# Around the expert loops of a two-layer trunk: fewer fill products, token sides made earlier, other closing sums

## The chip, the core and the metric

The kernel runs on one core of a Trainium2 chip. The metric is the device time in microseconds (us) of one execution, taken as the median over runs; lower is better.

## What is computed

The reference is a trunk of two layers over 512 tokens of width 1024, all in float32. Cut to what matters here:

```python
def reference(x, ...):
    x = x + sgu_mixer(rmsnorm(x, a_norm), ...)            # layer 0: gated MLP over 128-token blocks
    x = x + hierarchical_moe(rmsnorm(x, m_norm[0]), ...)  # 32 experts, two per token
    k, v, cum = shared_kv(x, kv_norm, kv_w, ...)          # keys, values, forget gates
    x = x + forgetting_attention(rmsnorm(x, b_norm), k, v, cum, ...)   # layer 1
    x = x + hierarchical_moe(rmsnorm(x, m_norm[1]), ...)
    return x

def expert_block(xb, e):                                  # inside hierarchical_moe
    hid = jax.nn.silu(xb @ w1[e]) * (xb @ w3[e])
    return hid @ w2[e]                                    # weighted, added to its tokens' rows
```

Each expert has three matrices of 2 MB (w1, w3, w2), so each layer reads 32 experts of 6 MB.

## The kernel before

`X` (128 partitions x 4 token blocks x 1024) holds the stream. The experts' weights go through three buffers `EB0` to `EB2`; an expert sits in buffer `slot(e)`. The loads of the first three experts are issued before a layer's expert loop. Every later one is issued by SyncE (SP) in `load_later_expert` (L403 to L415): w1 and w3 of expert e once the "up" products of the last item of expert e-3 are done, w2 once its "down" products are. SP waits in program order, and its transfers are served in that order.

An **item** is a slice of up to 32 tokens of one expert; there are 47 in each layer. TensorE runs `expert` (L1472) for each expert, with a loop over its items: up products (L1479), the sums of the item before into its tokens' rows (`move_items`, L1450), the gathering of the next item's tokens (L1468), down products (L1490). ScalarE does the silu (L663) and the weighted output `y_hi` (L666). VectorE multiplies and transposes (L986, L989), adds the moved rows to `X` (L995, `add_items`, which counts `added`), makes the next item's input (L959, L961), the **token sides** (`spread_tokens`, L968 and L971: zeros and ones that say which token rows an item's outputs go to; they are the stationary operand of L1450) and the rest `y_lo` of the weighted output (L1000).

Two places around this loop matter.

*Ahead of the loop* (VectorE, L974 to L983) the sides for token blocks 0 and 1 of the last items, `spread_end`, are made; then a memset counts `added` for the first time, and the loop starts. TensorE's first `move_items` waits for that count.

*After the loop* the outputs of the last two items are still to be added. TensorE's `move(banks, sides)` sums them for two token blocks into four banks (L1450, 32 products), first with `spread_end` for blocks 0 and 1, then with `spread` for blocks 2 and 3, which VectorE makes at L1021 after the last `add_items`. VectorE adds them to `X` (`add_moved`, L1029, counted by `x_moe`). In layer 0 the projection of the keys follows at once: its first weight tile `T_K` comes as one load of 2 MB into `ring[0]`, ScalarE splits it into a rounded part (L622, counted by `w_hi`) and VectorE into the rest (L853, counted by `w_lo`), in quarters; TensorE turns `X` (`turn_stream`, L1352), ScalarE and VectorE split the turned rows (`turned_hi`, L606; `rows_lo`, L843). In layer 1 the rows of blocks 2 and 3 are not added by VectorE: TensorE puts `X` into the banks by products with the identity (`rows_to_bank`, L1530, four column groups), sums on top of them, and ScalarE copies the two blocks out (L825). SP then stores the four blocks of `out` as each is ready (L463 to L466).

`keep_busy(bank, n)` is n products whose result nobody reads (the fill; each shows as two matmuls in the trace). There are 12 between the last-but-one expert and the last (L1526), 8 after the first closing `move` of layer 0 (L1541) and 8 more ahead of the projection of the keys (L1617).

## Time and profile before

| | |
|---|---|
| time, median of 3 runs | 1585.27 us (1583.48 to 1585.3) |
| span of the profiled execution | 1584.0 us |
| TensorE busy | 1476.6 us (93%) |
| VectorE busy | 980.7 us (62%) |
| ScalarE busy | 474.0 us (30%) |
| mean granted TensorE clock | 0.983 of full speed |
| DMA | 461.12 MB, mean 291 GB/s |

The span is the time from the first to the last instruction of one execution; what lies around it is not in it, and the profiled execution has no time of its own beside its span. The median of the timed runs is 1.3 us above that span. A clock of 1.00 in the rows is 2.4 GHz, 0.5 is 1.2 GHz.

### The profile page before, as it was taken

The numbers are of one execution on the slowest core, as the hardware profiler recorded it, in microseconds if no ns is written. First come the engines' busy times: TensorE is split into PE (matmuls) and PEld (weight loads), VectorE is DVE, ScalarE is ACT, GpSimd is POOL, SyncE is SP. The second block draws the span as 40 slices with busy tenths as digits, with TensorE's granted clock in tenths as the row PEclk, the third lists the DMA queues.
The fourth block names the chain that finished last, engine by engine and source line by source line (L and its number), as shares of the span: only waits on it lengthen the run. The fifth ranks groups of instructions, "written<-read, shape, count | busy, mean of one in ns | idle before, by whom it ended". The sixth has DMA issues, their size and how long they took to land.

```text
span 1584.0 us, 45784 instructions
## 1 busy us (share of the span) xinstructions
PE 1476.6 (93%) x18897; PEld 1002.0 (63%) x18898; DVE 980.7 (62%) x2114; ACT 474.0 (30%) x798; POOL 25.8 (2%) x64
## 2 busy tenths in 40 slices
PE   8999999999989989988999999989899897997978
PEld 6788888765555556545778875458655554554545
DVE  5346642377767767765744357852777675675755
ACT  6442221412222222221543355533222221221211
POOL 3000000000000000000000000000000000000000
PEclk9999999999999999998999999999999998999989
DMA  6331332989999999999431322125899999999996
GB/s 220 119 106 54 107 106 69 389 331 429 429 428 427 430 428 427 429 430 428 179 106 55 121 80 81 40 74 245 357 389 427 429 429 429 427 429 429 428 428 277
DMA packets 55482, 461.12 MB, mean 291 GB/s; under 512 B 4496, under 2 KB 4640, under 8 KB 30848
## 3 DMA queue, kind: packets, MB, share of 16 engines
q1 hardware_dynamic: 51728, 453.00, 69.0%
q10 hardware_dynamic: 2192, 4.23, 0.8%
q0 software_dynamic: 1504, 3.07, 0.7%
q8 instruction: 42, 0.69, 0.2%
q14 instruction: 16, 0.13, 0.0%
HBM read 458.15 MB, written 2.13 MB: 291 GB/s over the span
## 4 chain that ended last, share of the span: by engine, by line
PE 72%; DMA 22%; DVE 4%; issue 2%; SPq 0%; ACT 0%; DVEq 0%; ACTq 0%
DMA EB<-in_m_w 22%; PE ps L1479 15%; PE ps L1317 10%; PE ps L1319 10%; PE ps L1318 10%; PE ps L1468 7%; PE ps L1490 6%; PE ps L1450 4%; PE ps L1705 2%; PE ps L1740 1%; PE ps L1759 1%; PE ps L1774 1%; PE ps L1592 1%; PE ps L1313 1%; PE ps L1379 1%
## 5 line engine op out<-in xcount | busy, mean ns | idle before, releaser
L1479 PE MATMUL ps<-EB,SCR 128*32 128x256 f32 x6016 | 364.4, 397 | 72.5 <-DMA EB<-in_m_w 59.7
L1479 PEld LDWEIGHTS ps<-EB,SCR 128*32 128x32 f32 x6016 | 195.7, 114 | 233.4 <-issue 105.1
L995 DVE TENSOR_TENSOR X<-X,ps 128x1024 f32 x188 | 221.1, 1218 | 28.9 <-PE ps L1450 28.9
L1319 PE MATMUL ps<-EB_r 128*128 128x512 f32 x512 | 200.2, 391 | 0.0
L1468 PE MATMUL ps<-H,SCR 128*32 128x256 f32 x3072 | 185.6, 382 | 0.0
L1490 PE MATMUL ps<-EB,SCR 128*32 128x256 f32 x3008 | 179.5, 379 | 0.0
L666 ACT ACTIVATE SCR_r<-ps,SCR 128x256 f32 x94 | 44.5, 474 | 443.4 <-PE ps L1490 443.4
L986 DVE TENSOR_TENSOR SCR<-SCR,ps 128x128 f32<-128x128 f32 x94 | 37.0, 393 | 211.6 <-ACT SCR L663 211.6
L1490 PEld LDWEIGHTS ps<-EB,SCR 128*32 128x32 f32 x3008 | 97.7, 110 | 64.5 <-DVE SCR L989 0.4
L1318 PE MATMUL ps<-EB_r 128*128 128x512 f32 x352 | 137.5, 391 | 0.0
L1468 PEld LDWEIGHTS ps<-H,SCR 128*32 128x32 f32 x3072 | 90.4, 110 | 62.1
L1317 PE MATMUL ps<-EB_r,H_r 128*128 128x512 f32 x320 | 126.8, 396 | 1.4 <-DVE EB L1084 1.0
L1450 PEld LDWEIGHTS ps<-SCR_r 32*128 32x128 f32 x3136 | 99.8, 184 | 44.6 <-issue 44.6
L1318 PE MATMUL ps<-EB_r,H_r 128*128 128x512 f32 x320 | 124.7, 390 | 0.0
L1450 PE MATMUL ps<-SCR_r 32*128 32x256 f32 x3136 | 119.6, 290 | 3.7 <-DVE col L983 2.1
L663 ACT ACT_TABLE_LOAD x94 | 120.6, 1283 | 2.0 <-ACT SCR L659 0.3
L1319 PEld LDWEIGHTS ps<-EB_r 128*128 128x128 f32 x512 | 96.3, 188 | 20.5
L663 ACT ACTIVATE SCR<-ps 128x128 f32<-128x128 f32 x94 | 26.1, 278 | 245.3 <-PE ps L1479 245.3
L971 DVE SCALAR_TENSOR_TENSOR SCR_r<-SCR,item_slot,SCR_r 128x256 fp32r<-128x256 f32 x192 | 84.6, 482 | 14.8 <-DVE SCR_r L968 14.7
L857 DVE TENSOR_TENSOR EB_r<-EB,EB_r 128x1024 fp32r<-128x1024 f32 x56 | 65.1, 1220 | 38.2 <-ACT EB_r L625 38.2
L1317 PE MATMUL ps<-EB_r 128*128 128x512 f32 x192 | 77.4, 403 | 3.6 <-DVE EB_r L1288 3.5
L1318 PEld LDWEIGHTS ps<-EB_r 128*128 128x128 f32 x352 | 66.5, 189 | 12.6
(280 smaller groups left out, 1667.0 us busy)
## 6 DMA issues: line engine op xcount, KB each, us to landing
EB<-in_m_w SPq DMA_DIRECT2D x192, 2048.0 KB, 26.9
EB<-in_a_w_in SPq DMA_DIRECT2D x7, 2048.0 KB, 8.2
EB<-in_a_w_out SPq DMA_DIRECT2D x4, 2048.0 KB, 7.9
EB<-in_kv_w SPq DMA_DIRECT2D x4, 2048.0 KB, 12.6
EB<-in_b_w_qg SPq DMA_DIRECT2D x4, 2048.0 KB, 7.9
EB<-in_b_w_out SPq DMA_DIRECT2D x2, 2048.0 KB, 9.4
X<-in_x SPq DMA_DIRECT2D x4, 512.0 KB, 6.9
EB<-in_a_w_in SPq DMA_DIRECT2D x4, 512.0 KB, 9.7
```

The lines of the kernel that those rows point to most:

```text
L663: a.activation(silu, ps[0][:, 0:P], ACT.Silu).then_inc(m["silu"], 1)
L666: a.activation(y_parts[:, bass.ds(n & 1, 1), 0, :], ps[2][:, CW:2 * CW].unsqueeze(1), ACT.Copy, scale=slot_w[:, bass.ds(n, 1)]).then_inc(m ...
L857: v.tensor_tensor(ring_lo[j][:, 2 * q:2 * q + 2, :], ring[j][:, 2 * q:2 * q + 2, :], ring_hi[j][:, 2 * q:2 * q + 2, :].bitcast(F32), ALU.s ...
L971: v.scalar_tensor_tensor(dst[:, i, :], toks[1], item_slot[:, bass.ds(items[i] + 2, 1)], dst[:, i, :].bitcast(F32), ALU.is_equal, ALU.add). ...
L995: add = v.tensor_tensor(X_t, X_t, moved[1][:, :, t, :], ALU.add)
L1317: mm(o, left[0], right[0], start=start, stop=False)
L1318: mm(o, left[0], right[1], start=False, stop=False)
L1319: return mm(o, left[1], right[0], start=False, stop=stop)
L1450: last = mm(moved[banks][:, g, t, :], sides[rows, i, t * P:(t + 1) * P], y_parts[rows, i, k, :], start=first and i == 0 and k == 0, stop=( ...
L1468: last = mm(ps[1][g * CAP:(g + 1) * CAP, 0:CW], S[:, c, :], H[:, c * D + g * CW:c * D + (g + 1) * CW], start=c == 0, stop=c == NT - 1)
L1479: last = mm(ps[0][g * CAP:(g + 1) * CAP, 0:2 * P].rearrange("p (w n) -> p w n", w=2), xT[:, k, :], w13_sb[s][:, :, k, g * P:(g + 1) * P], ...
L1490: last = mm(ps[2][g * CAP:(g + 1) * CAP, CW:2 * CW], hidT[:, c, :], w2_sb[s][:, c, g * CW:(g + 1) * CW], start=c == 0, stop=c == KE - 1)
```

## The change

Six edits go together. (1) The fill ahead of the last expert has 2 products where it had 12, and the fill after layer 0's first closing `move` 6 where it had 8. (2) The sides for blocks 2 and 3 are made ahead of the loop, behind `spread_end`, into a place of their own (`spread_late`, in the buffer `gain`). (3) In layer 0 VectorE adds block 0 only after the first quarter of `T_K`'s rest, and block 1 only after the rest of block 0's turned rows. (4) `T_K` comes in four loads of 512 KB, each with its own semaphore. (5) In layer 1 the first closing `move` goes to the other four banks and no longer waits for `added`; only two column groups of blocks 2 and 3 are put into banks by identity products, and the other two are added by VectorE while ScalarE copies the first out. (6) Blocks 2 and 3 are stored by column halves.

```diff
+        spread_late = gain_r[:, 0:2 * CW].rearrange("p (i n) -> p i n", i=2)
...
-            for i in range(T_K, T_K + 2):
-                sp.dma_start(ring[i % 2], tiles[i]).then_inc(tile_loaded[i % 2], 16)
+            for q in range(4):
+                sp.dma_start(ring[0][:, 2 * q:2 * q + 2, :], tiles[T_K][:, 2 * q:2 * q + 2, :])\
+                    .then_inc(first_loaded[q], 16)
+            sp.dma_start(ring[1], tiles[T_K + 1]).then_inc(tile_loaded[1], 16)
...
-            for t in range(NT):
-                sp.wait_ge(*((x_moe, NT + t + 1) if t < 2 else (x_copied, t - 1)))
+            for t in range(2):
+                sp.wait_ge(x_moe, NT + t + 1)
                 sp.dma_start(out[0, t * P:(t + 1) * P, :], X[:, t, :]).then_inc(stored, 16)
+            for h, ready in ((1, (x_copied, 1)), (0, (x_moe, NT + 3))):
+                sp.wait_ge(*ready)
+                sp.dma_start(out[0, 2 * P:T, h * COL:(h + 1) * COL].rearrange("(t p) n -> p t n", p=P),
+                             X[:, 2:4, h * COL:(h + 1) * COL]).then_inc(stored, 16)
...
             act.wait_ge(end_moved, 4)
-            for t in range(2):
-                a.activation(X[:, 2 + t, :].rearrange("p (g n) -> p g n", g=CG), moved[0][:, :, t, :], ACT.Copy)\
-                    .then_inc(x_copied, 1)
+            a.activation(X[:, 2:4, COL:D].rearrange("p t (g n) -> p g t n", g=2), moved[1][:, 2:4], ACT.Copy)\
+                .then_inc(x_copied, 1)
...
                 spread_tokens(spread_end, 0, (total - 2 + (total & 1), total - 1 + (total & 1)), lambda ins, i: then(ins),
                               end_spread)
+                spread_tokens(spread_late, 1, (total - (total & 1), total - 2 + ((total + 1) & 1)),
+                              lambda ins, i: then(ins), end_spread)
                 dve.wait_ge(slot_w_done, 2 * l + 2)
                 v.memset(cn[:, 0:1], 0.0).then_inc(m["added"], 1)
...
                 add_items(total - 1)
-                spread_tokens(spread, 1, (total - (total & 1), total - 2 + ((total + 1) & 1)), lambda ins, i: then(ins),
-                              end_spread)
                 rest_of_rows(total - 1)
...
                 dve.wait_ge(end_moved, 2 * l + t // 2 + 1)
+                if l == 1 and t == 2:
+                    X_g = X[:, 2:4, 0:COL].rearrange("p t (g n) -> p g t n", g=2)
+                    v.tensor_tensor(X_g, X_g, moved[1][:, 0:2], ALU.add).then_inc(x_moe, 1)
+                    return
...
-            for t in range(2):
-                add_moved(0, t)
             split_tile(T_K, 0, 1)
+            add_moved(0, 0)
             rows_lo("kv", 0)
+            add_moved(0, 1)
             split_tile(T_K, 1, 4)
...
-                keep_busy(0, 12, CW)
+                keep_busy(0, 2, CW)
                 expert(slot(NE - 1), (NE - 1) // NBUF + 1, start_of(NE - 1), total, True)
...
-                pe.wait_ge(m["added"], total + 1)
-                if l == 1:
-                    for g in (0, 1, 3):
-                        rows_to_bank(g)
+                if l == 0:
+                    pe.wait_ge(m["added"], total + 1)
+                pe.wait_ge(end_spread, 4 * l + 4)
                 pe.wait_ge(m["y_hi"], total + 1)
                 pe.wait_ge(m["y_lo"], total + 1)
-                pe.wait_ge(end_spread, 4 * l + 2)
-                move(1, spread_end).then_inc(end_moved, 1)
+                move(1 - l, spread_end).then_inc(end_moved, 1)
                 if l == 0:
-                    keep_busy(0, 8)
+                    keep_busy(0, 6)
                     turn_stream(0)
                     pe.wait_ge(x_moe, 2)
-                if l == 1:
-                    rows_to_bank(2)
-                pe.wait_ge(end_spread, 4 * l + 4)
-                move(1 - l, spread, first=l == 0).then_inc(end_moved, 1)
+                    move(1, spread_late).then_inc(end_moved, 1)
+                    return
+                pe.wait_ge(m["added"], total + 1)
+                for g in range(2, CG):
+                    mm(moved[1][:, g, :, :], ident[:, :], X[:, 2:4, g * CW:(g + 1) * CW], start=True, stop=False)
+                move(1, spread_late, 2).then_inc(end_moved, 1)
```

Three places in the order of instructions show what moves (after the change line numbers are 14 to 18 higher). VectorE ahead of layer 0's loop, before the change:

```order
L968 TENSOR_SCALAR SCR_r<-SCR,item_slot 128x256
L968 ISA [waits dve_step]
L968 TENSOR_SCALAR SCR_r<-SCR,item_slot 128x256
L971 SCALAR_TENSOR_TENSOR SCR_r<-SCR,item_slot,SCR_r 128x256 [waits dve_step]
L971 SCALAR_TENSOR_TENSOR SCR_r<-SCR,item_slot,SCR_r 128x256
L983 MEMSET col 128x1 [waits slot_w_done]
```

The same place after the change:

```order
L985 SCALAR_TENSOR_TENSOR SCR_r<-SCR,item_slot,SCR_r 128x256
L982 ISA
L982 TENSOR_SCALAR gain_r<-SCR,item_slot 128x256
L982 REGISTER_ALU [waits dve_step]
L982 REGISTER_ALU
L982 ISA
L982 TENSOR_SCALAR gain_r<-SCR,item_slot 128x256
L985 SCALAR_TENSOR_TENSOR gain_r<-SCR,item_slot,gain_r 128x256 [waits dve_step]
L985 SCALAR_TENSOR_TENSOR gain_r<-SCR,item_slot,gain_r 128x256
L999 MEMSET col 128x1 [waits slot_w_done]
```

Four more instructions, with two waits of VectorE on itself, stand between `spread_end` and the memset that TensorE waits for. VectorE behind layer 0's loop, before (from the sides after the last `add_items` on; L853 is the weight tile's rest, L843 the turned rows'):

```order
L968 TENSOR_SCALAR SCR_r<-SCR,item_slot 128x256
L971 SCALAR_TENSOR_TENSOR SCR_r<-SCR,item_slot,SCR_r 128x256 [waits dve_step]
L971 SCALAR_TENSOR_TENSOR SCR_r<-SCR,item_slot,SCR_r 128x256
L1000 ISA [waits moe0_y_hi]
L1000 ISA
L1000 SCALAR_TENSOR_TENSOR SCR_r<-ps,SCR,SCR_r 128x256
L1029 TENSOR_TENSOR X<-X,ps 128x1024 [waits end_moved] x2
L853 SCALAR_TENSOR_TENSOR EB_r<-EB,cols,EB_r 128x512 [waits w_hi]
L853 SCALAR_TENSOR_TENSOR EB_r<-EB,cols,EB_r 128x512
L843 TENSOR_TENSOR EB_r<-ps,H_r 128x4x128 [waits kv_ht] x2
```

And after:

```order
L1016 SCALAR_TENSOR_TENSOR SCR_r<-ps,SCR,SCR_r 128x256
L867 SCALAR_TENSOR_TENSOR EB_r<-EB,cols,EB_r 128x512 [waits w_hi]
L867 SCALAR_TENSOR_TENSOR EB_r<-EB,cols,EB_r 128x512
L1047 TENSOR_TENSOR X<-X,ps 128x1024 [waits end_moved]
L857 TENSOR_TENSOR EB_r<-ps,H_r 128x4x128 [waits kv_ht] x2
L1047 TENSOR_TENSOR X<-X,ps 128x1024 [waits end_moved]
```

The sides are gone; the add of block 1 now stands behind the rest of block 0's turned rows. TensorE at the end of layer 1, before:

```order
L1530 MATMUL ps<-X,ident 128x512 [waits moe1_added]
L1530 MATMUL ps<-X,ident 128x512 x2
L1450 MATMUL ps<-SCR_r 128x256 [waits end_spread,moe1_y_lo,moe1_y_hi]
L1450 MATMUL ps<-SCR_r 128x256 x31
L1530 MATMUL ps<-X,ident 128x512
L1450 MATMUL ps<-SCR_r 128x256 [waits end_spread]
L1450 MATMUL ps<-SCR_r 128x256 x31
```

And after:

```order
L1550 REGISTER_ALU [waits end_spread]
L1468 MATMUL ps<-SCR_r 128x256 [waits moe1_y_lo,moe1_y_hi]
L1468 MATMUL ps<-SCR_r 128x256 x31
L1561 MATMUL ps<-X,ident 128x512 [waits moe1_added]
L1561 MATMUL ps<-X,ident 128x512
L1468 MATMUL ps<-SCR_r,gain_r 128x256 x32
```

Two of four identity products are gone, and the first closing sums stand ahead of them.

## Rows read from the trace of the kernel before

**Rows 1.** Page, chain of work that ended last: shares of the span by engine

```profile
PE 72%; DMA 22%; DVE 4%; issue 2%; SPq 0%; ACT 0%; DVEq 0%; ACTq 0%
```

**Rows 2.** Timeline, layer 0's loop opening: start, us, engine, line, operands, count [idle before]

```profile
325.92 0.35 DVE L968 TENSOR_SCALAR SCR_r<-SCR,item_slot 128x256 fp32r<-128x256 f32 x1 [0.34 <-DVE SCR L979]
...
326.94 0.88 DVE L971 SCALAR_TENSOR_TENSOR SCR_r<-SCR,item_slot,SCR_r 128x256 fp32r<-128x256 f32 x2
...
327.99 1.22 PE L1450 MATMUL ps<-SCR_r 32*128 32x256 f32 x32 [1.07 <-DVE col L983]
```

**Rows 3.** Stretches: us, busy PE PEld DVE ACT POOL, PEclk, DMA share, GB/s

```profile
344.00:346.00 2.00, 2.00 (x48) 1.18 (x40) 0.77 (x3) 0.37 (x2) 0.00 (x0) 1.00 0.04 16
```

**Rows 4.** DMA issues at 345.75, 717.84, 721.99, 749.71, 1529.67: KB, us to landing

```profile
EB<-in_m_w SPq DMA_DIRECT2D x1, 2048.0 KB, 7.4
...
EB<-in_m_w SPq DMA_DIRECT2D x1, 2048.0 KB, 38.2
...
EB<-in_m_w SPq DMA_DIRECT2D x1, 2048.0 KB, 39.0
...
EB<-in_kv_w SPq DMA_DIRECT2D x1, 2048.0 KB, 16.8
...
EB<-in_m_w SPq DMA_DIRECT2D x1, 2048.0 KB, 37.7
```

**Rows 5.** Timeline, layer 0's last expert and the handover to the keys

```profile
754.32 2.94 PE L1313 MATMUL ps<-tri_in,tri 128*128 128x128 f32 x24
...
762.03 1.93 PE L1490 MATMUL ps<-EB,SCR 128*32 128x256 f32 x32
...
764.29 0.47 ACT L666 ACTIVATE SCR_r<-ps,SCR 128x256 f32 x1 [3.09 <-PE ps L1490]
...
766.39 0.48 DVE L1000 SCALAR_TENSOR_TENSOR SCR_r<-ps,SCR,SCR_r 128x256 f32 x1
766.51 2.56 ACT L622 ACTIVATE EB_r<-EB,cols 128x512 fp32r<-128x512 f32 x4 [1.75 <-DMA EB<-in_kv_w]
...
767.28 1.22 PE L1450 MATMUL ps<-SCR_r 32*128 32x256 f32 x32 [1.59 <-DVE SCR_r L1000]
...
768.55 2.35 DVE L1029 TENSOR_TENSOR X<-X,ps 128x1024 f32<-128x1024 f32 x2 [1.69 <-PE ps L1450]
...
770.32 1.04 PE L1352 MATMUL ps<-ident,X 128*128 128x128 f32 x8
...
770.82 1.41 DVE L853 SCALAR_TENSOR_TENSOR EB_r<-EB,cols,EB_r 128x512 fp32r<-128x512 f32 x2
...
771.29 1.22 PE L1450 MATMUL ps<-SCR_r 32*128 32x256 f32 x32
```

**Rows 6.** Timeline, a later block turned on TensorE and its rest on VectorE

```profile
782.73 1.04 PE L1352 MATMUL ps<-ident,X 128*128 128x128 f32 x8
...
783.99 1.29 DVE L843 TENSOR_TENSOR EB_r<-ps,H_r 128x512 fp32r<-128x512 f32 x2 [0.43 <-ACT H_r L606]
```

**Rows 7.** Timeline, end of layer 1

```profile
1567.57 1.94 PE L1490 MATMUL ps<-EB,SCR 128*32 128x256 f32 x32
...
1571.16 2.84 PE L1530 MATMUL ps<-X,ident 128*128 128x512 f32 x6
...
1575.08 1.13 PE L1530 MATMUL ps<-X,ident 128*128 128x512 f32 x2
...
1576.45 3.25 SPq L465 DMA_DIRECT2D out_x<-X  x4
...
1577.41 1.94 ACT L825 ACTIVATE X<-ps 128x1024 f32<-128x1024 f32 x2 [7.11 <-PE ps L1450]
```

**Rows 8.** Timeline of TensorE, up products after three waits for weights

```profile
682.78 3.66 PE L1479 MATMUL ps<-EB,SCR 128*32 128x256 f32 x64 [3.31 <-DMA EB<-in_m_w]
...
726.82 6.23 PE L1479 MATMUL ps<-EB,SCR 128*32 128x256 f32 x64 [4.89 <-DMA EB<-in_m_w]
...
1445.13 5.35 PE L1479 MATMUL ps<-EB,SCR 128*32 128x256 f32 x64 [3.32 <-DMA EB<-in_m_w]
```

**Rows 9.** Stretch behind the wait that ends at 726.82, columns as in rows 3

```profile
725.00:730.00 5.00, 3.18 (x32) 1.62 (x36) 0.00 (x0) 0.00 (x0) 0.00 (x0) 0.53 1.01 429
```

More of the change, by code:

```diff
@@ L84, in trunk @@
         SCR, SCR_r = sb_split("SCR", [P, 5 * D])
-        gain = sb("gain", [P, D])
+        gain, gain_r = sb_split("gain", [P, D])
         h_tok = H[:, :].rearrange("p (t g k r) -> p t g k r", t=NT, g=CG, k=KD)
@@ L348, in split_no, with tile_loads @@
             return i if i <= T_G else i - (T_WO - T_G - 1)
+        def tile_loads(i):
+            if i == T_K:
+                return None
+            return i // 2 + i % 2 - (i % 2 == 0 and i > T_K)
         H_LO = {"a": 0, "kv": 2 * NT}
@@ L616, in split_hi @@
             def split_hi(j, loads, q0=0, q1=4, scale=None):
-                act.wait_ge(tile_loaded[j], 16 * loads)
+                if loads is not None:
+                    act.wait_ge(tile_loaded[j], 16 * loads)
                 for q in range(q0, q1):
+                    if loads is None:
+                        act.wait_ge(first_loaded[q], 32)
                     if scale is not None:
@@ L628, in split_tile @@
             def split_tile(i, q0=0, q1=4):
-                split_hi(i % 2, i // 2 + i % 2, q0, q1, weight_gain(i))
+                split_hi(i % 2, tile_loads(i), q0, q1, weight_gain(i))
             def moe_act(l, ready):
@@ L750, in scale_gate @@
             def scale_gate(i, k):
-                act.wait_ge(tile_loaded[i % 2], 16 * (i // 2 + i % 2))
+                act.wait_ge(tile_loaded[i % 2], 16 * tile_loads(i))
                 a.activation(ring[i % 2][:, k, :], ring[i % 2][:, k, :], ACT.Copy, scale=b_gain[:, k:k + 1])\
@@ L1027, in add_moved @@
                 dve.wait_ge(end_moved, 2 * l + t // 2 + 1)
+                if l == 1 and t == 2:
+                    X_g = X[:, 2:4, 0:COL].rearrange("p t (g n) -> p g t n", g=2)
+                    v.tensor_tensor(X_g, X_g, moved[1][:, 0:2], ALU.add).then_inc(x_moe, 1)
+                    return
                 X_t = X[:, t, :].rearrange("p (g n) -> p g n", g=CG)
-                v.tensor_tensor(X_t, X_t, moved[1 - l * (t // 2)][:, :, t % 2, :], ALU.add).then_inc(x_moe, 1)
+                v.tensor_tensor(X_t, X_t, moved[1 - l][:, :, t % 2, :], ALU.add).then_inc(x_moe, 1)
             def router_blocks(l, add):
@@ L1302, in _ @@
             moe_dve(1)
-            for t in range(2):
+            for t in range(3):
                 add_moved(1, t)
@@ L1441, in moe_pe, with move @@
                    start=False, stop=True).then_inc(lists_out, 1)
-                def move(banks, sides, first=True):
+                def move(banks, sides, opened=CG):
                     for t in range(2):
@@ L1450, in move @@
                                     last = mm(moved[banks][:, g, t, :], sides[rows, i, t * P:(t + 1) * P],
-                                              y_parts[rows, i, k, :], start=first and i == 0 and k == 0,
-                                              stop=(first or t == 1) and i == 1 and k == 1)
+                                              y_parts[rows, i, k, :], start=g < opened and i == 0 and k == 0,
+                                              stop=(g < opened or t == 1) and i == 1 and k == 1)
                     return last
@@ L1525, in moe_pe @@
                 total = pe.value_load(n0_i[0:1, NE:NE + 1], min_val=NE, max_val=MAX_ITEMS)
-                keep_busy(0, 12, CW)
+                keep_busy(0, 2, CW)
                 expert(slot(NE - 1), (NE - 1) // NBUF + 1, start_of(NE - 1), total, True)
-                def rows_to_bank(g):
-                    mm(moved[0][:, g, :, :], ident[:, :], X[:, 2:4, g * CW:(g + 1) * CW], start=True, stop=False)
-                pe.wait_ge(m["added"], total + 1)
-                if l == 1:
-                    for g in (0, 1, 3):
-                        rows_to_bank(g)
+                if l == 0:
+                    pe.wait_ge(m["added"], total + 1)
+                pe.wait_ge(end_spread, 4 * l + 4)
                 pe.wait_ge(m["y_hi"], total + 1)
                 pe.wait_ge(m["y_lo"], total + 1)
-                pe.wait_ge(end_spread, 4 * l + 2)
-                move(1, spread_end).then_inc(end_moved, 1)
+                move(1 - l, spread_end).then_inc(end_moved, 1)
                 if l == 0:
-                    keep_busy(0, 8)
+                    keep_busy(0, 6)
                     turn_stream(0)
                     pe.wait_ge(x_moe, 2)
-                if l == 1:
-                    rows_to_bank(2)
-                pe.wait_ge(end_spread, 4 * l + 4)
-                move(1 - l, spread, first=l == 0).then_inc(end_moved, 1)
+                    move(1, spread_late).then_inc(end_moved, 1)
[4 more added lines that the diff above has]
+                move(1, spread_late, 2).then_inc(end_moved, 1)
             pe.wait_ge(const_ready, 5)
```

## The prediction

> **What bounds the kernel now.** I read the chain of waits first, and in it the share of each engine: 72% TensorE and 22% DMA [rows 1]. That mixes two regimes, so I went to the expert loops and listed every weight load with its issue and landing. The reader is to see three things there. First, the loads run dry once, near the start: in 344 to 346 us the DMA engines are 4% busy [rows 3], because the load of the fifth expert's w1 is issued only at 345.75, when TensorE has freed its buffer, and lands at 353.1. Second, from there on they never run dry: 28 experts follow with three loads each, and the last, w2, is issued at 721.99 and lands 39.0 later, at 761.0 [rows 4]. That is 83 steps in 407.9 us, 4.9 us for each 2 MB, without a hole. Third, TensorE is a little faster than that and waits again and again for weights (waits of 3.3 to 4.9 us in [rows 8]). So between 345.75 and the last expert the loop is bound by the stream of loads. What delays 345.75 delays the end of the layer by as much, and work saved on TensorE inside buys nothing. Layer 1 has the same pattern: its last w2 lands at 1529.67 + 37.7 = 1567.4 and the last down products start at 1567.57 [rows 4, 7]. Between the loops, and ahead of 345.75, TensorE is the bound.
>
> **The change part by part**, in the times of the profiled execution.
>
> *Sides made ahead of the loop.* `spread_end` takes VectorE from 325.92 to 327.82, 1.9 us for four instructions, and TensorE's first `move_items` starts at 327.99, held by the memset behind them [rows 2]. The new four have the same shapes and the same waits on themselves, so 1.9 us more stand ahead of that memset. Behind it on VectorE wait the first item's hidden products (L986) and so the down products too; nothing in this stretch hides them, since TensorE already waited 1.07 us there. TensorE is 1.9 us late at 345.75, and the stream of loads, dry at that moment, starts 1.9 us late. Cost +1.9 in each layer. Bounds: 0 if something ahead of 345.75 took it up, 2.3 if the registers for the items' numbers add to it.
>
> *Fill ahead of the last expert, layer 0.* 24 matmuls take 2.94 us from 754.32 on [rows 5]; 20 of them go, 2.45 us. But w3 of this expert, issued at 717.84, lands at 756.0, and w2 at 761.0 [rows 4]; both are now 1.9 later. The fill would end at 754.3 + 1.9 + 0.5 = 756.7, the up products wait for w3 until 758.0 (they began at 757.2), and the down products for w2 until 763.0, where they began at 762.03 [rows 5]. Net +0.95: of the 2.45 us saved 0.95 arrive.
>
> *Sides gone behind the loop.* y_hi ends at 764.76 + 0.95 = 765.7, and the rest L1000 follows it at once, at 765.75 where it stood at 766.39 behind the sides. The first closing move starts 0.65 earlier, at 766.65 [rows 5].
>
> *Handover to the keys.* The first quarter of `T_K` must be split before VectorE adds block 0. The whole tile lands 16.8 after 749.71, at 766.5, 5.5 behind w2 [rows 4]; a quarter takes 1.4, so the first is there at 761.0 + 1.4 + 1.9 = 764.3 and does not hold ScalarE, which is busy until 765.7. ScalarE's two pieces take half of 2.56, to 767.1; VectorE's two 1.41, to 768.5; the add of block 0 half of 2.35, to 769.7 [rows 5], the very time of before. TensorE turns block 0 at 769.8 to 770.1, before at 770.32 because of the fill. From the start of such turning to the end of VectorE's rest of the turned rows it takes 782.73 to 785.28, 2.55 us [rows 6]: 772.3 to 772.6. Only now comes the add of block 1, 1.2 more, and 0.4 behind it the second closing move (before: add ended 770.90, move 771.29 [rows 5]): 773.9 to 774.2. The eight fill products and the keys follow as before. So the keys start 2.6 to 2.9 us late, I take +2.7; this is the sum of layer 0 with its opening in it. The two fill products taken out are worth nothing: TensorE waits for the add instead. The later quarters, blocks and loads keep their cover, the keys' products, which start late themselves; of five SP issues in place of two none is waited for.
>
> *Last expert of layer 1.* Its down products start 0.17 after w2 lands: the fill was worth nothing there, 0 to -0.1.
>
> *End of layer 1.* Four identity products (eight matmuls) take 2.84 + 1.13 = 3.97 [rows 7]; two go: TensorE ends 1.95 earlier, near 1575.4. ScalarE copies once where it copied twice, 1.94 in all, so its half is out near 1576.4. VectorE adds blocks 0 and 1 from 1572.5 to 1574.8 and its half of the others from 1575.4 to 1576.6. The last store was issued at about 1576.45 + 3.25 - 0.35 = 1579.35; now near 1577.0. Gain 2.3; bounds 1.9 (TensorE's part alone) and 2.9 (with all of one copy). Rows of 2 KB where they were 4 KB are inside these bounds: `T_K` comes in rows of 2 KB at 5.5 us for 2 MB against 4.9, 0.15 for a store of 512 KB.
>
> *The clock.* In the handover TensorE now stands idle from about 769.3 to 769.9 and from 770.9 to 774.0, 3.6 us in 4.7, with eight short products between. After a wait of 3.31 us the up products took 3.66 us, after one of 3.32 they took 5.35, and after one of 4.89 they took 6.23 [rows 8]; behind that last one the granted clock is 0.53 over 5 us, so nearly all of it at 1.2 GHz [rows 9]. A fall costs 1.7 to 2.6 us where TensorE is the bound. I take one fall, in the handover, at the smaller price, 1.7, because the products behind this gap are long and dense. At each loop opening the wait grows from 1.07 to 3.0 us, shorter than both the 3.31 that kept the clock and the 3.32 that lost it; I leave the clock up there. Ahead of layer 1's last expert the 2.45 us of fill turn into idle time, shorter still.
>
> The rows put the fall here by the length of the gap alone. The Trainium skill ("TensorE: Matmul & The Clock Gate", section "Why this matters for your kernels") asks that idle gaps between bursts of products be kept short, since otherwise the half clock comes back; it speaks against taking fill away at all. By it the handover and perhaps both openings fall: +2.3 + 3 x 1.7 = +7.4. By the row that kept the clock none falls: +2.3. The trace shows both sides of it, one wait of 3.31 kept and one of 3.32 lost.
>
> **Sum.** +2.7 (layer 0) + 1.9 (opening of layer 1) + 0 (last expert) - 2.3 (end) = +2.3; with the fall +4.0. Against the span of 1584.0 that is 1588.0; the median of the runs shown stands 1.3 above the span, so 1589.3.
>
> **The rivals.**
> *More falls of the clock* (0.22): an opening falls too. For it: 3.0 us of idle is near 3.3. Against it: both examples are longer. With one more +5.7, 1591.0; with two +7.4, 1592.7.
> *No fall* (0.16): for it the wait of 3.31. +2.3, 1587.6.
> *The openings are hidden* (0.10; the other side). If the 1.9 us do not reach the issue at 345.75, the last w2 lands at 761.0 as before, the down products start 0.9 earlier instead of later, and the keys start at +0.8; then +0.8 + 0 - 2.3 = -1.5, with a fall +0.2: 1583.8 to 1585.5. It decides from where less than about half of the 1.9 arrives at 345.75. Against it: TensorE has no idle time to give between 329 and 345 but the wait for VectorE.
> *The handover costs nothing and the openings little* (0.09): VectorE's new order overlaps better than the rows say; down to -4, 1581.3.
> *As forecast* (0.40): 1588.0 to 1590.5. About 0.03 is left for none of these.
>
> **How the numbers follow.** What a measurement of this kernel can tell from no change is about 0.2%, 3.2 us. Slower by more: most of the forecast (0.33), more falls (0.22), a little of no fall (0.03) and of the rest (0.02): 0.60. Within: the remainder of the forecast (0.07), of no fall (0.13), the hidden openings and the rest (0.11): 0.31. Faster: 0.09. The range 1585.3 to 1592.2 leaves out the faster cases and the case of three falls; the likeliest case's own range is 1588.0 to 1590.5.
>
> **What would show it.** Right: VectorE's first loop memset about 1.9 us later after `spread_end`, the load that ended the dry stretch 1.9 us later against the loop's start, landings 4.9 us apart up to the end; TensorE waiting for a DMA ahead of both last experts; an idle stretch of about 3 us between the turning of block 0 and the second closing move in layer 0, and half clock behind it; four identity matmuls less and the last store about 2.3 us earlier against layer 1's last down products. Wrong: the issue near 345.75 at its old distance from the loop's start, a second closing move in layer 0 not later than before, or a gain at the end under 1.9 or over 2.9.

## The result, and the profile after

The changed kernel takes 1595.09 us (median of 4 runs, 1589.9 to 1598.76), the kernel before beside it 1584.65 (1583.48 to 1585.3): ratio 1.0064, 95% interval 1.0052 to 1.0076. In the first group of experiments it was 1593.65 against 1584.65, ratio 1.0055 (1.0042 to 1.0069). It is slower by 10.4 us here and by 9.0 there, where the prediction said 4 and ended its range at 1592.2. The profiled execution took 1589.9 us, with a span of 1588.1; it is the fastest of the four, which matters below.

The end of the page's chain of waits, shares by engine (before: [rows 1]), shows more time behind transfers and less behind TensorE:

```profile
PE 68%; DMA 25%; DVE 4%; issue 2%; ACT 0%; SPq 0%; DVEq 0%; ACTq 0%
```

Timeline of the changed kernel at the opening of layer 0's loop (start, us, engine, line, operands, count, idle before), first VectorE, then TensorE:

```profile
327.02 0.88 DVE L985 SCALAR_TENSOR_TENSOR SCR_r<-SCR,item_slot,SCR_r 128x256 fp32r<-128x256 f32 x2
327.82 0.34 DVE L982 TENSOR_SCALAR gain_r<-SCR,item_slot 128x256 fp32r<-128x256 f32 x1
...
328.88 0.88 DVE L985 SCALAR_TENSOR_TENSOR gain_r<-SCR,item_slot,gain_r 128x256 fp32r<-128x256 f32 x2
...
329.71 0.06 DVE L999 MEMSET col<- 128x1 f32 x1
```

```profile
323.34 3.66 PE L1497 MATMUL ps<-EB,SCR 128*32 128x256 f32 x64
329.93 2.08 PE L1468 MATMUL ps<-SCR_r 32*128 32x256 f32 x32 [2.93 <-DVE col L999]
331.94 2.42 PE L1486 MATMUL ps<-H,SCR 128*32 128x256 f32 x32
...
336.88 3.66 PE L1497 MATMUL ps<-EB,SCR 128*32 128x256 f32 x64 [0.79 <-issue]
```

The second set of sides (`gain_r`) lies between 327.82 and 329.76, and the memset behind it (L999) ends at 329.77, where it ended at 327.83 before: 1.9 us, as predicted. TensorE's first `move_items` starts at 329.93 after 2.93 us of idle time ([rows 2]: 1.07). It takes 2.08 us and the gather behind it 2.42, where 1.22 and 1.93 are usual: the clock fell. The stretch 329 to 334 shows it (granted clock 0.66), and the DMA share of 346 to 349 (0.00) shows the dry loads, which restart at 349.04 instead of 345.75 (columns as in [rows 3]; the DMA share and GB/s come last):

```profile
346.00:349.00 3.00, 3.00 (x64) 1.67 (x54) 1.95 (x6) 1.47 (x3) 0.00 (x0) 1.00 0.00 0
329.00:334.00 5.00, 4.07 (x64) 2.92 (x68) 3.10 (x7) 0.00 (x0) 0.00 (x0) 0.66 0.92 393
```

The opening of layer 1, with nearly the same idle time (2.92 us), kept the clock. The last row is the last expert of layer 1, whose up products waited 2.39 us for w3 behind the two fill products and took 5.35 us, partly at half clock, instead of 3.66; before, they stood behind the fill without such a wait:

```profile
1139.85 1.22 PE L1468 MATMUL ps<-SCR_r 32*128 32x256 f32 x32 [2.92 <-DVE col L999]
...
1567.87 5.35 PE L1497 MATMUL ps<-EB,SCR 128*32 128x256 f32 x64 [2.39 <-DMA EB<-in_m_w]
```

Handover of layer 0, TensorE and VectorE (before: [rows 5]):

```profile
764.48 1.93 PE L1508 MATMUL ps<-EB,SCR 128*32 128x256 f32 x32
...
769.79 1.21 DVE L1047 TENSOR_TENSOR X<-X,ps 128x1024 f32<-128x1024 f32 x1
...
771.06 1.09 PE L1370 MATMUL ps<-ident,X 128*128 128x128 f32 x8 [0.18 <-DVE X L1047]
...
772.45 1.29 DVE L857 TENSOR_TENSOR EB_r<-ps,H_r 128x512 fp32r<-128x512 f32 x2 [1.44 <-ACT H_r L618]
...
773.65 1.21 DVE L1047 TENSOR_TENSOR X<-X,ps 128x1024 f32<-128x1024 f32 x1
...
774.92 1.22 PE L1468 MATMUL ps<-SCR_r,gain_r 32*128 32x256 f32 x32 [2.77 <-DVE X L1047]
```

Block 0 is added in 769.79 to 771.00, turned, its rest made to 773.74, and only then is block 1 added (to 774.86). The second closing move (L1468 at 774.92) waited 2.77 us for it, and the keys start at 777.88, 13.40 behind the down products (before 12.21). The end of layer 1, whose down products start at 1574.38 (before: [rows 7]):

```profile
1579.19 1.98 PE L1561 MATMUL ps<-X,ident 128*128 128x512 f32 x4
...
1581.10 1.22 PE L1468 MATMUL ps<-SCR_r,gain_r 32*128 32x256 f32 x32
1582.38 1.02 ACT L839 ACTIVATE X<-ps 128x1024 f32<-128x1024 f32 x1 [5.25 <-PE ps L1468]
1582.38 1.22 DVE L1044 TENSOR_TENSOR X<-X,ps 128x1024 f32<-128x1024 f32 x1 [0.72 <-PE ps L1468]
```

One group of identity products of 1.98 us stands where 3.97 stood, one copy (L839) where two stood. From the down products to the end of the span it is 13.67 us, before 16.48.

### The profile page after: what moved, and what is told of

Same layout as the page of the kernel before. It is cut to its first block, busy times and chain, and to the rows that moved or that the text cites. A ratio compares the mean times of both kernels' runs of the same rounds, so it can differ in the third digit from the quotient of the medians.

```text
span 1588.1 us, 45690 instructions
## 1 busy us (share of the span) xinstructions
PE 1474.6 (93%) x18849; PEld 998.2 (63%) x18850; DVE 982.2 (62%) x2115; ACT 473.1 (30%) x797; POOL 25.9 (2%) x64
## 4 chain that ended last, share of the span: by engine, by line
PE 68%; DMA 25%; DVE 4%; issue 2%; ACT 0%; SPq 0%; DVEq 0%; ACTq 0%
DMA EB<-in_m_w 25%; PE ps L1497 14%; PE ps L1335 10%; PE ps L1337 10%; PE ps L1336 10%; PE ps L1486 6%; PE ps L1508 5%; PE ps L1468 4%; PE ps L1720 2%; PE ps L1755 1%; PE ps L1774 1%; PE ps L1789 1%; PE ps L1607 1%; PE ps L1397 1%; PE ps L1383 0%
## 5 line engine op out<-in xcount | busy, mean ns | idle before, releaser
L1468 PEld LDWEIGHTS ps<-SCR_r 32*128 32x128 f32 x3072 | 98.7, 185 | 46.6 <-issue 46.6
L1468 PE MATMUL ps<-SCR_r 32*128 32x256 f32 x3072 | 118.4, 291 | 6.7 <-DVE col L999 5.8
```

The costliest lines, as they stand in the source:

```text
L1468: last = mm(moved[banks][:, g, t, :], sides[rows, i, t * P:(t + 1) * P], y_parts[rows, i, k, :], start=g < opened and i == 0 and k == 0, s ...
```

## Where the time is, stretch by stretch

All traces were cut at the same points of the timeline: "start" is layer 0's first up products; "opening" from there to the second item's; "last" from the landing of the last w2 to the last down products; "handover" from these to the first keys product; "keys" from there to layer 1's first up products; "end" from layer 1's last down products to the end of the span. The first row is the kernel before in us, the others the difference to it. Not shown is the loop from the second item to the last landing: 427.05 to 427.51 us in all 20 traces and both layers. So the loop took the same time whatever stood around it, and never carried a difference.

| trace | start | opening 0 | last 0 | handover | keys | opening 1 | last 1 | end | span |
|---|---|---|---|---|---|---|---|---|---|
| before | 323.26 | 10.33 | 1.04 | 12.21 | 355.42 | 10.28 | 0.20 | 16.48 | 1584.0 |
| after, profiled | +0.1 | +3.2* | -1.0 | +1.2 | 0 | +1.8 | +1.6* | -2.8 | +4.0 |
| r1_after | +0.2 | +3.3* | +0.6* | +2.8* | +1.0 | +1.8 | +1.6* | -2.8 | +7.9 |
| r2_after | +1.1 | +3.5* | +0.7* | +2.8* | +1.1 | +1.8 | 0 | -2.8 | +7.9 |
| r3_after | +1.0 | +3.5* | +0.7* | +2.8* | +1.2 | +1.9 | +1.6* | -2.8 | +9.4 |
| r4_after | +0.8 | +3.4* | +0.7* | +2.8* | +1.0 | +1.8 | 0 | -2.8 | +7.6 |
| e1_sides | +1.0 | +3.4* | -0.9 | -0.9 | +0.1 | +3.6* | 0 | 0 | +6.1 |
| e2_fills | +0.7 | 0 | +0.7* | -0.5 | +1.1 | 0 | -0.1 | 0 | +1.5 |
| e3_end | -0.4 | 0 | 0 | -0.2 | -1.6 | 0 | 0 | -1.3 | -3.9 |
| e4_order | +1.1 | 0 | -0.9 | +5.4* | -1.6 | 0 | 0 | 0 | +3.6 |
| e5_back_sides | +1.3 | -0.1 | -0.9 | +2.1 | -1.7 | 0 | +1.5* | -1.5 | +0.5 |
| e6_back_order | +0.6 | +3.4* | +0.7* | -1.9 | 0 | +3.4* | +1.6* | -2.8 | +4.7 |
| e7_back_fill | +1.0 | +3.5* | -0.9 | +3.7* | +0.2 | +3.4* | 0 | -2.8 | +7.7 |
| e8_mem | +1.0 | -0.1 | +0.7* | +2.6* | 0 | -0.1 | +1.6* | -2.8 | +2.3 |
| e11_open_fill | +1.5 | +1.8 | -0.9 | +2.7* | +1.3 | +1.9 | +1.5* | -2.8 | +6.8 |
| e13_fill_and_order | +0.4 | +3.3* | -0.9 | -1.9 | -1.7 | +3.5* | 0 | -2.8 | -0.7 |
| e10_best | +0.4 | -0.1 | -0.9 | -1.9 | -1.6 | -0.1 | 0 | -2.8 | -7.6 |
| e12_best_sides_back | +1.4 | -1.2 | -0.9 | -0.6 | +1.1 | -1.2 | +1.0 | -1.5 | -2.1 |
| e14_sides_in_gap | +0.8 | -1.1 | -0.9 | -1.9 | +1.2 | -1.2 | +1.0 | -2.8 | -4.8 |
| e15_sides_in_gap_8 | +0.4 | -1.2 | -0.9 | -1.9 | +1.2 | -1.2 | +0.8 | -2.8 | -5.9 |

A star: the clock fell in that stretch (in "end", where it falls in every trace once TensorE is done, none is set). "Start" and "keys" lie outside the change and move by up to 1.5 and 1.7 us in kernels of every kind; what moves "keys" is a fall near 1056 us that is absent (353.8 us), short (355.4) or twice as long (356.5). So the parts are read in the other columns, with the medians as a check on them. Each row is one execution. In "last 0" the -0.9 needs no edit: e4 has it too, whose code is that of the kernel before up to there, and so have e1, e7, e10 and e13 with all 12 fill products. The traces of before and e3 are the ones in which TensorE came 1.0 us late for the last w2.

## The experiments

Theory A: the mechanism of the prediction holds, and the clock falls at more places than one. Its rival in the first group, B: the stream of loads itself runs slower than before. Later rivals stand with their runs. "Before" stands at 1584.6 to 1585.0 us in every group of runs.

**The whole change and its parts, each alone on the kernel before.**

> The changed kernel again, to see how wide its own times are and where a slower execution loses. Theory A (late loop openings, late handover): the profiled spans scatter with the number of falls of the TensorE clock, 1.2 to 1.7 us each, at five places (both openings, both last experts, the handover): 1588 to 1594 us of device time. Theory B (something outside the changed places is slower, such as the rate of the loads): the last weight load of a layer lands more than 408 us after the first one behind the dry stretch, and times reach 1599.

> The kernel before with the sides of blocks 2 and 3 made ahead of the loop, nothing else. Theory A: the loads restart 1.9 us later in each layer, layer 0 gives 1.6 back behind its loop, layer 1 nothing: +2.2 us with the clock up, up to +6 with a fall at each opening. Rival (the openings are hidden): 0 to -1.6 us. Theory B': the fills alone make the loss: this one is within 1 us of before.

> The kernel before with the shorter fills alone (12 to 2, 8 to 6). Theory A: layer 0 gains 0.9 to 1.2 us (the rest of the removed 2.45 us is a wait for weights), layer 1 nothing: -1.2 to -0.9 us with the clock up. Theory B' (the fills held the clock up): +1 to +5 us, the spread of times wider than before, low clock over the last expert's products.

> The kernel before with layer 1's closing sums, copies and stores of the change alone. Theory A: -2.3 us (bounds -1.9 and -2.9). Rival: the four stores bunch and the last lands no earlier: 0 to -1.

e1 adds the two parts of the diff on `spread_late`, e2 is `keep_busy(0, 2, CW)` and `keep_busy(0, 6)`, e3 edits (5) and (6). Measured: r1 1593.65; e1 1591.12, ratio 1.0036 (1.0023 to 1.005); e2 1586.86, 1.001 (1.0001 to 1.0019); e3 1582.71, 0.9988 (0.9979 to 0.9997). The sides alone bring +6.5 us, the fills +2.2, the end -1.9. B falls: the loop between the second item and the last landing takes the same in all. e1 came out half a us above A's range, with a fall at each opening. e2 contradicts A (-1.2 to -0.9) and fits its rival, that the fills held the clock: its trace has one fall at the touched places, in layer 0's last expert, after a wait of 2.17 us. The touched stretches of that trace sum to only +0.1, though; the rest of its +1.5 lies mostly in "start" and "keys", so e2 does not show how much of the +2.2 the fill makes. e3 is at the edge of A's bounds by its time (-1.9), but in its trace the end gains only 1.3. In the changed kernel it gains 2.8, because the sides no longer stand in its way: in e3 the first closing sum, which now goes ahead of the identity products, stands idle for 1.24 us and starts (1569.91) once VectorE has made `y_lo` (1569.81) behind the sides; before, the identity products covered that. So the sides ahead are worth 1.5 at the end once the closing sums are the new ones, and cost 7 at the openings (e1; 5.2 on average in the changed kernel).

The order of VectorE alone is the fourth part:

```diff
-            for t in range(2):
-                add_moved(0, t)
             split_tile(T_K, 0, 1)
+            add_moved(0, 0)
             rows_lo("kv", 0)
+            add_moved(0, 1)
```

> The kernel before with one part only, VectorE's order at the handover (the first key quarter's low part, the add of block 0, the turned rows, the add of block 1). Theory A: the second closing sum starts 2.6 to 3.2 us later behind the first's, down products to the first keys product 14.3 to 15.3 us where they took 12.21, more by 1.5 with a fall of the clock: 1587 to 1589 us. Rival (the keys' start moves, but the later key tiles are reached by their loads at the same time, so that it is given back): the keys start later and layer 1's loop starts as before, 1585.0 us.

1589.6 us, ratio 1.0031 (1.0019 to 1.0043), a little above A. Handover 17.58 us, 5.4 more than before, with a fall in it. Layer 1's first up products start 3.9 us later than before, so it is not given back. The handover is also longer than A's 15.3 plus 1.5: in this trace ScalarE waits 2.53 us for `T_K`, which still comes as one load here, and the add of block 0 stands behind its first quarter. In the changed kernel, where `T_K` comes in four loads, ScalarE does not wait there. No run tests edit (4), the four loads, by itself. Timeline of e4_order, TensorE:

```profile
767.17 1.22 PE L1450 MATMUL ps<-SCR_r 32*128 32x256 f32 x32 [1.33 <-DVE SCR_r L1000]
...
771.41 1.09 PE L1352 MATMUL ps<-ident,X 128*128 128x128 f32 x8 [1.04 <-DVE X L1029]
775.27 2.03 PE L1450 MATMUL ps<-SCR_r 32*128 32x256 f32 x32 [2.77 <-DVE X L1029]
777.23 2.77 PE L1313 MATMUL ps<-tri_in,tri 128*128 128x128 f32 x16
```

**Each part undone in the changed kernel.** e5 makes the late sides behind `add_items(total - 1)` again, e6 restores the old order above, e7 is

```diff
-                keep_busy(0, 2, CW)
+                keep_busy(0, 12, CW)
```

and e8 leaves all work in place but lets TensorE go first:

```diff
+                dve.wait_ge(slot_w_done, 2 * l + 2)
+                v.memset(cn[:, 0:1], 0.0).then_inc(m["added"], 1)
                 spread_tokens(spread_end, 0, (total - 2 + (total & 1), total - 1 + (total & 1)), lambda ins, i: then(ins),
                               end_spread)
                 spread_tokens(spread_late, 1, (total - (total & 1), total - 2 + ((total + 1) & 1)),
                               lambda ins, i: then(ins), end_spread)
-                dve.wait_ge(slot_w_done, 2 * l + 2)
-                v.memset(cn[:, 0:1], 0.0).then_inc(m["added"], 1)
```

> The changed kernel, but the sides of blocks 2 and 3 (kept in the gain's tile) are made behind the last item's adds again, as before. Theory A (the sides ahead of the loop make a wait of about 2.9 us in each opening, which costs 1.8 us and in most executions 1.5 us more for the lost clock): both openings come back to 10.3 us from first to second up products, that is 3.3 to 6.9 us less; the last second sides then stand ahead of the closing sums again, 0.7 us at the handover and up to 1.5 us at the end; in all 1587 to 1590 us. Rival B (fewer fill products and the new order of VectorE carry the loss): 1591 to 1594 us.

> The changed kernel, with VectorE's order at the handover as before (two closing adds, then the first key quarter's low part and the rows). Down products of the last expert to the first keys product took 14.98 and 13.40 us with the new order and 6 fill products, 11.36 us with the old order, 8 fill products and sides ahead. If the order causes it: 11.4 to 12.0 us there and 1590.5 to 1592 us in all. If the two fill products less cause it: it stays at 13.4 to 15.0 and the time stays within 0.5 us of the changed kernel's 1593.65.

> The changed kernel with 12 fill products ahead of the last expert instead of 2. Theory A: the wait of 2.4 us for the last first half loses the clock in the last expert of either layer in most executions (up products 5.35 us instead of 3.7), with the fills back the down products start 0.2 us after the last load in layer 1 and at most 1.0 in layer 0: 0.7 to 2.5 us less, 1591.2 to 1593 us. Rival: those products are hidden behind the load either way, no change from 1593.65.

> The changed kernel, but VectorE's memset, which releases the first item's moved rows on TensorE, stands ahead of both makings of sides instead of behind them. Theory A (what costs in the opening is TensorE's wait for that release): TensorE goes from the up products to the move and the next gather without a gap, no fall of the clock there, openings at 10.3 to 12.1 us and the whole at 1587 to 1590.5 us. Rival (VectorE's own 1.9 us delays the first item's hidden rows): openings stay at 12.1 us and only the clock's part comes back, 1590 to 1592.5.

The differences here are to r1's 1593.65, which was measured in another group. e5 1587.62 (ratio 1.002, 1.0009 to 1.0031): openings back, -6.0 us. e6 1589.38 (1.0022, 1.0013 to 1.0032): -4.3, below the 1590.5 to 1592 expected; the handover takes 10.28, so the order costs 3.1 us there without a fall (13.40) and 4.7 with one (14.98), and the two fill products less are no part of it. Timeline of e6_back_order, TensorE: the second move follows the turning without a wait.

```profile
770.11 1.22 PE L1468 MATMUL ps<-SCR_r 32*128 32x256 f32 x32
771.26 1.60 PE L1331 MATMUL ps<-tri_in,tri 128*128 128x128 f32 x12
772.70 1.05 PE L1370 MATMUL ps<-ident,X 128*128 128x128 f32 x8
773.79 1.22 PE L1468 MATMUL ps<-SCR_r,gain_r 32*128 32x256 f32 x32
```

e8 1588.1 (1.0012, 1.0003 to 1.0021): -5.6 us. Both openings are at 10.2 with VectorE's eight instructions still there. Timeline of e8_mem, TensorE, layer 0:

```profile
324.21 3.66 PE L1497 MATMUL ps<-EB,SCR 128*32 128x256 f32 x64
327.80 1.22 PE L1468 MATMUL ps<-SCR_r 32*128 32x256 f32 x32
328.95 1.93 PE L1486 MATMUL ps<-H,SCR 128*32 128x256 f32 x32
331.32 1.93 PE L1508 MATMUL ps<-EB,SCR 128*32 128x256 f32 x32 [0.43 <-DVE SCR L1005]
334.40 3.66 PE L1497 MATMUL ps<-EB,SCR 128*32 128x256 f32 x64 [1.15 <-DVE SCR L975]
```

The rival, that VectorE's own 1.9 us delay the hidden rows, falls as it stood: what costs the 1.8 us and the fall is TensorE's wait for the memset. Once TensorE may go ahead, the move and the gather (3.1 us) cover most of VectorE's work. What is left are TensorE's waits for VectorE in these rows (0.43 and 1.15 us); where the second sides are not ahead of the loop and the memset stands first (e12), the opening takes 9.1, so they still cost 1.1 there.

e7 missed: 1593.4 (1.0054, 1.0039 to 1.0068), where 1591.2 to 1593 was expected. The last experts did come back (-0.9 and 0), but the clock now fell in layer 1's opening and for longer in the handover. A rival remained, that these products are worth nothing; e13 restores order and fill together, so that nothing falls behind them. Beside it stand three more traces of the changed kernel.

> The changed kernel with VectorE's old order at the handover and 12 fill products ahead of the last expert; against the run with the old order alone (1589.38 us) it tells what the 10 products are worth where nothing falls behind them. Theory A: their removal costs 0.7 us in layer 0 and 1.6 in layer 1 through the clock, so 1587.0 us (1586.3 to 1588). Rival (with them put back, the changed kernel came to 1593.4 and not to 1591.4, so they are worth nothing): 1589.4 us.

> The changed kernel again, one trace more. In two traces of it the clock fell in two openings of four, in the handover once of two, and in the last expert three times of four. If falls are what stands between the profiled 1589.9 and the median of 1593.65: about 3 to 4 falls at these five places, 1592 to 1596 us, each fall dearer by 1.2 to 1.8 us than the same stretch without one.

> The changed kernel, a fourth trace: 3 to 4 falls of the clock at the five places (two openings, two last experts, the handover), 1592 to 1596 us; with fewer falls it should be nearer 1590.

> The changed kernel, a fifth trace: 3 to 4 falls of the clock at the five places (two openings, two last experts, the handover), 1592 to 1596 us; with fewer falls it should be nearer 1590.

e13 1587.86 (1.002, 1.0011 to 1.0029), 1.5 below e6: inside A's range, though smaller than its 2.4. The intervals of the two overlap, so the times alone do not decide against the rival; the traces do, since the up products of both last experts take 5.35 us in e6 and 3.66 in e13. In all 20 traces the clock never fell in a last expert behind 8 or 12 fill products (20 cases), and it fell in 14 of 20 cases behind 2. The three further traces came to 1593.73, 1595.24 and 1593.48 with 3, 4 and 3 falls at the five places, against 2 in the profiled 1589.9. Stretches of r3_after behind three of its falls (opening, last expert, handover):

```profile
331.00:336.00 5.00, 5.00 (x76) 3.01 (x80) 3.04 (x5) 0.00 (x0) 0.00 (x0) 0.66 1.00 423
761.00:766.00 5.00, 5.00 (x64) 2.69 (x60) 0.00 (x0) 0.09 (x1) 0.00 (x0) 0.66 0.98 390
778.00:783.00 5.00, 5.00 (x44) 4.74 (x38) 3.39 (x6) 1.11 (x2) 0.00 (x0) 0.66 0.00 0
```

**Is it the idle time or the moment?** e11 lays fill into the openings' wait (`fill` is 10 for the first expert, 0 for the others), with everything else as it is:

```diff
                         last.then_inc(m["up"], 1)
+                        if fill:
+                            pe.wait_ge(m["y_hi"], n + 1)
+                            pe.wait_ge(m["y_lo"], n + 1)
+                            keep_busy(2, fill, CW)
                         move_items(n)
```

> The changed kernel with 10 fill products (2.45 us) laid into the wait that the second sides made in each opening, in a bank that nobody reads there, behind the first expert's up products. VectorE's work and the wait's end stay as they are. Theory A (the opening costs 1.8 us for VectorE's four instructions and 1.5 us more because TensorE's idle time of 2.9 us loses the clock): both openings take 12.1 us from first to second up products with no fall of the clock, where they took 13.5 to 13.9 in most traces; 1590.3 to 1592.3 us. Rival (the clock falls there whether TensorE is idle or not): openings stay at 13.5 us, no change from 1593.65.

1592.03 (1.004, 1.0027 to 1.0054), 1.6 under r1 but with overlapping intervals; the trace is clearer, though it is one. Both openings take 12.15 and keep the clock, where layer 0's lost it in all nine traces that have the bare wait of 2.9 us; the wait for the memset (+1.8) stays. Timeline of e11_open_fill, TensorE, layer 0:

```profile
324.73 3.66 PE L1497 MATMUL ps<-EB,SCR 128*32 128x256 f32 x64
328.32 2.50 PE L1331 MATMUL ps<-tri_in,tri 128*128 128x128 f32 x20
331.32 1.22 PE L1468 MATMUL ps<-SCR_r 32*128 32x256 f32 x32 [0.50 <-DVE col L999]
332.47 1.93 PE L1486 MATMUL ps<-H,SCR 128*32 128x256 f32 x32
```

**A version that keeps what was good.** e10 is the changed kernel with the edits of e6, e7 and e8 together; e12 is e10 with e5's. e14 is e10 with both sets of sides moved from ahead of the loop to

```diff
                     select(n + 2, m, 0, lambda ins, k: link(ins, k + 2))
+                spread_tokens(spread_end, 0, (total - 2 + (total & 1), total - 1 + (total & 1)), lambda ins, i: then(ins),
+                              end_spread)
+                spread_tokens(spread_late, 1, (total - (total & 1), total - 2 + ((total + 1) & 1)),
+                              lambda ins, i: then(ins), end_spread)
                 gate_item(total - 1)
```

and e15 has `keep_busy(0, 8, CW)` there besides.

> The changed kernel with the three losses taken out: the memset ahead of both sides, 12 fill products ahead of the last expert again, and VectorE's old order at the handover; the sides ahead of the loop, 6 fill products at the handover and the new end of layer 1 stay. Theory A, by the stretches measured so far: openings 10.2 us (as before), last experts as before, down products to keys 10.3 us (1.9 less), end 13.7 us (2.8 less): 4.7 us under the kernel before, 1580.3 us, between 1579.5 and 1581.5. Rival (the parts hide one another's cost, and the gain at the handover comes back as a wait for the key tiles): 1582.2 us, the end's gain alone.

> The kernel of the run before this one (label e10_best), but with the sides of blocks 2 and 3 made behind the last adds again. If those sides ahead of the loop are worth something once the opening doesn't wait for them: handover 0.7 us longer and end 1.5 us longer than there, 1582.0 to 1583.0 us. Rival: within 0.5 us of it.

> The kernel of label e10_best, but all eight instructions that make the four sides stand behind the expert loop on VectorE, ahead of the last item's hidden rows, where VectorE waits 4.1 to 4.4 us for ScalarE (from 755.9 to 760.3 in e10_best's trace; eight instructions take 3.8). Theory A (the sides cost only where somebody waits): openings 9.1 us as with one set behind (1.1 less than in e10_best), handover and end as in e10_best; in layer 1 about 1.0 of it is given back at the last expert, where TensorE with its 12 fill products is itself late for the load; 1578.0 to 1579.8 us. Rival: the hidden rows of the last expert come late behind them, 1580.5 or more.

> As label e14_sides_in_gap, with 8 fill products ahead of the last expert instead of 12. Theory A: the four products less (0.98 us) end the fill about when the last first half has landed in layer 1, so 0.5 to 1.0 us less than e14_sides_in_gap, 1577.3 to 1579 us, with the clock up because the idle time there stays under 1.5 us. Rival: the shorter fill loses the clock in the last expert as 2 products do, 0.7 to 1.6 us more.

e10 1580.54 (0.9972, 0.9962 to 0.9983), as A summed it. e12 1581.75 (0.9981, 0.9972 to 0.999): between the two; by the traces the sides ahead win 1.3 us at handover and end each and lose 1.1 at each opening, but in layer 1 that loss costs next to nothing, since in e12 its last expert stands 1.0 longer behind the load. The intervals of e10 and e12 overlap.

e14 1580.97 (0.9975, 0.9964 to 0.9986) missed its range by 1.2. The openings gained 1.1 each and layer 1's last expert gave 1.0 back, with TensorE late for its own loads, both as expected; against e10's trace the touched stretches sum to -1.0. But its median is 0.4 above e10's, and no run shows why: what is longer in its trace are "start" (0.4), the two loops (0.5) and "keys" (2.9), none of which the edit touches. e15 1578.82 (0.996, 0.9946 to 0.9973) has the lowest median, 5.9 us under before, with an interval that overlaps those of e10 and e14. Its trace has no fall in an opening, a last expert or the handover. Of the 1.0 in layer 1's last expert only 0.2 came back: TensorE is no longer late there, but its down products wait 0.61 us for VectorE's hidden rows, which stand behind the sides. So the rival of e14 is partly true here, and the four products less explain little of the 2.1 us between the two medians.

Timeline of e14_sides_in_gap, VectorE, where it waited 4.36 us in e10's trace:

```profile
756.13 0.35 DVE L982 TENSOR_SCALAR SCR_r<-SCR,item_slot 128x256 fp32r<-128x256 f32 x1 [0.18 <-issue]
...
760.05 0.40 DVE L998 TENSOR_TENSOR SCR<-SCR,ps 128x128 f32<-128x128 f32 x1 [0.17 <-ACT SCR L678]
```

## Why the prediction was wrong

*The bound, right.* From the second item to the last landing it took 427 us in every trace, so what delays the loads' restart delays the layer.

*Openings, half right.* +1.9 for VectorE's four instructions: measured +1.8 where the clock stayed (layer 1, five of five traces). e8 shows this to be TensorE's wait for the memset. The step that failed is the clock's: "At each loop opening the wait grows from 1.07 to 3.0 us, shorter than both the 3.31 that kept the clock and the 3.32 that lost it; I leave the clock up there." The wait was 2.93 and lost the clock in layer 0 in all five traces of the changed kernel, 1.4 to 1.6 us more each; e11, which fills the wait, keeps it.

*Last experts, wrong in the same way.* +0.95 net in layer 0 and 0 in layer 1 took the waits for w3 as harmless (of layer 1's: "shorter still"). They were 2.2 to 2.5 us where TensorE was not late already, and behind each of those the up products took 5.35 us. In layer 0 the forecast had a wait of 1.3 (756.7 to 758.0): with the fall in the opening the loads came 3.2 to 3.5 us later, not 1.9, while the fill ended where the forecast had it (r1: 756.9). The stretch "last" ended at +0.6 or +0.7 in layer 0 in four of five traces, where -1.0 was forecast, and at +1.6 in layer 1 in three of five. The fill's 12 products had been holding the clock, which the forecast credited with nothing. The -1.0 itself was read from one trace in which TensorE came late; e4 has 0.9 of it with the fill of before.

*Handover, right in kind, somewhat too dear.* Forecast +1.75 and +3.45 with a fall; measured +1.2 and +2.8. The fall taken there came in four of five. The wait for block 1's add was 2.77 us, and 0.2 ahead of the turning. Part of the excess is the 0.4 us put between block 1's add and the second closing move: it was 0.06 (774.86 to 774.92). In the row it was taken from, the move had followed the turning and had not waited for the add.

*End, right.* Forecast -2.3, bounds -1.9 and -2.9; measured -2.8. The last store was issued 2.2 us earlier against the down products, as forecast; the other 0.6 lie between that issue and the end of the span. The forecast holds for the closing sums and the earlier sides together: with the sides still behind the loop it is -1.3 (e3).

*The price of a fall*, 1.7 where TensorE is the bound: measured 1.5 (opening, 13.54 against 12.08), 1.6 (handover, 14.98 against 13.40), 1.6 (last expert), so nearly right. Their number was wrong: one was taken, the five traces have 2, 4, 3, 4 and 3.

In sum over the five traces (means): openings +3.37 and +1.82, last experts +0.34 and +0.95, handover +2.47, end -2.81 make +6.14, where the forecast had +4.0. Another 1.2 us (start, keys and the rest, 7.4 in all) lies in stretches that the change does not touch, and no run here shows whether it comes from the change; falls there move from kernel to kernel. By the times of these five executions (mean 1593.2 us against the median of 1584.65) the change costs 8.6 us; what separates that from 7.4 stays open, since there is one trace of the kernel before. The profiled execution alone would have looked like a hit, +4.0 on the span, but by luck: it has two falls where none was forecast and none where one was.

The Trainium skill ("TensorE: Matmul & The Clock Gate", section "Why this matters for your kernels") says to keep idle gaps between bursts short. The prediction weighed its rule as a rival with two or three falls; the traces side with its direction, and it applied to the last experts too. The gap that the section's table names is longer than the 2.08 to 2.47 us that lost the clock there; where the two differ, the measurement decides.

Open: why the same wait of 2.92 us in layer 1's opening never fell in the changed kernel but did in e1, e6, e7 and e13. This wasn't separated from what TensorE did before.

## What to carry to other kernels

Work that is put ahead of a release is paid by whoever waits for the release: signal first, then do the work (the memset ahead of both sides was worth 5.6 us, clock included), or place it where its engine waits anyway, as far as the gap holds it. Fill products ahead of a transfer that bounds the loop look worthless in a sum of durations, but what they hold is the clock; in this kernel 35 of the 44 waits of 2.05 to 2.94 us at these places lost it, mostly at 1.4 to 1.6 us each, so such a wait is to be counted as a probable fall and not as free. And one profiled execution tells one outcome of such falls: take several traces before sizing an edit by them.

## What the runs showed of the hardware

Of the waits for w3 ahead of a last expert with 2 fill products, those of 0.79, 0.93, 0.99, 1.24, 2.05 and 2.06 us kept the clock, and fourteen from 2.08 to 2.47 lost it, without an exception. Yet 2.92 kept it five times and lost it four in layer 1's opening, and 2.77 in the handover kept it twice and lost it eight times of ten, and 3.31 kept it in [rows 8]. The length of a gap alone does not decide. With the old order in the handover, which has no such wait, none of ten traces shows a fall there. Which later waits fell also differed from kernel to kernel (layer 1's opening in e7, but not in r1); no run separates why. The parts alone come to 6.5 + 2.2 + 4.7 - 1.9 = 11.5 us, together to 9.0; the intervals of the parts are too wide for that difference to show anything. The stretches do show that parts lean on each other: at the end the new sums alone gain 1.3 and the sides alone 0, together 2.8.
